# Spectral heads by a real transform's symmetry, and five low parts by transfers that add

## The reference, cut to what matters

```python
p = h @ w_in_ab[e]                        # 1024 -> 512 spectral + 512 conv + 512 gate
a4 = a.reshape(1, 256, 4, 128)            # 256 tokens, 4 heads of 128 features
f = jnp.fft.fft2(a4, axes=(1, 3), norm="ortho").real
y = jnp.einsum("bshd,hde->bshe", f, fnet_map)
```

## Time and profile before

| | us |
|---|---|
| median of 3 runs | 734.05 |
| lowest, highest | 733.32, 734.15 |
| span of the profiled execution, first to last instruction | 731.6 |
| run's median less that span | 2.45 |
| PE busy | 719.8 (98%) |
| DVE busy | 502.8 (69%) |
| ACT busy | 395.2 (54%) |
| POOL busy | 2.4 |

### The profile page before, as it was taken

One profiled execution on the slowest core, in us unless ns is written; L12 is line 12 of the kernel. 1 busy time (PEld: TensorE's weight loads), 2 busy tenths in 40 slices (PEclk: granted clock), 3 DMA queues, 4 the chain that ended last, 5 costly groups with the idle time before them and its releaser, 6 DMA issues.

```text
span 731.6 us, 9776 instructions
## 1 busy us (share of the span) xinstructions
PE 719.8 (98%) x3940; PEld 629.7 (86%) x3940; DVE 502.8 (69%) x801; ACT 395.2 (54%) x614; POOL 2.4 (0%) x8
## 2 busy tenths in 40 slices
PE   7999999999999999999999999999999999999996
PEld 6888889999999999888888888888888888888885
DVE  5879996998877889977744555555686445555544
ACT  3167446874886675658644434443666444344423
POOL 0000000000000000000000000000000000000000
PEclk9999999999999999999999999999999999999999
DMA  8999994798835343423755545554336555455201
GB/s 329 416 422 422 421 410 154 259 396 327 325 124 212 135 161 116 179 102 116 288 177 197 201 173 180 206 190 172 116 116 229 176 198 200 173 181 207 73 1 57
DMA packets 23085, 156.13 MB, mean 213 GB/s; under 512 B 2560, under 2 KB 2816, under 8 KB 5120
## 3 DMA queue, kind: packets, MB, share of 16 engines
q1 hardware_dynamic: 22464, 152.88, 55.2%
q0 software_dynamic: 576, 2.62, 0.9%
HBM read 154.44 MB, written 1.05 MB: 213 GB/s over the span
## 4 chain that ended last, share of the span: by engine, by line
PE 87%; DVE 6%; DMA 4%; ACT 2%; SPq 1%; issue 0%; ACTq 0%
PE pb L1601 22%; PE pb L1603 22%; PE pb L1602 21%; PE pb L1665 10%; DMA raw<-w_dram 4%; DVE raw L1032 3%; DVE w L1029 2%; PE pb L1894 2%; PE pb L2005 1%; PE pb L1758 1%; PE pb L1757 1%; PE pb L1759 1%; PE pb L2073 1%; PE pb L1927 1%; PE pb L1937 0%; PE pb L1872 0%
## 5 line engine op out<-in xcount | busy, mean ns | idle before, releaser
L1029 DVE TENSOR_TENSOR w<-raw,w 128x2048 fp32r<-128x2048 f32 x97 | 221.4, 2291 | 141.2 <-ACT w L629 141.2
L629 ACT ACTIVATE w<-raw 128x2048 fp32r<-128x2048 f32 x97 | 184.9, 1915 | 138.7 <-PE pb L1603 114.7
L1601 PE MATMUL pb<-w,r 128*128 128x512 f32 (+1 forms) x640 | 244.6, 382 | 0.0
L1603 PE MATMUL pb<-w,r 128*128 128x512 f32 (+1 forms) x640 | 241.1, 377 | 0.0
L1602 PE MATMUL pb<-w,r 128*128 128x512 f32 (+1 forms) x640 | 240.7, 376 | 0.0
L1603 PEld LDWEIGHTS pb<-w,r 128*128 128x128 f32 x640 | 120.4, 188 | 22.6
L1601 PEld LDWEIGHTS pb<-w,r 128*128 128x128 f32 x640 | 120.6, 188 | 21.2 <-issue 0.2
L1602 PEld LDWEIGHTS pb<-w,r 128*128 128x128 f32 x640 | 120.6, 188 | 21.0
L1601 PE MATMUL pb<-r,w 128*128 128x256 f32 x288 | 82.5, 287 | 0.4 <-DVE r L1029 0.4
L1603 PE MATMUL pb<-r,w 128*128 128x256 f32 x288 | 81.5, 283 | 0.0
L1602 PE MATMUL pb<-r,w 128*128 128x256 f32 x288 | 81.5, 283 | 0.0
(11 more groups left out here) (208 smaller groups left out, 673.6 us busy)
## 6 DMA issues: line engine op xcount, KB each, us to landing
raw<-w_dram SPq DMA_DIRECT2D x129, 1024.0 KB, 4.9
ow<-w_dram SPq DMA_DIRECT2D x8, 1024.0 KB, 15.3
ow<-w_dram SPq DMA_DIRECT2D x8, 512.0 KB, 16.9
oh<-w_dram SPq DMA_DIRECT2D x2, 1024.0 KB, 22.5
x<-x_dram SPq DMA_DIRECT2D x2, 512.0 KB, 5.3
f<-rc_dram POOLq DMA_DIRECT2D x1, 1024.0 KB, 5.6
acc<-row_dram POOLq DMA_DIRECT2D x2, 512.0 KB, 6.7
out_dram<-f SPq DMA_DIRECT2D x4, 256.0 KB, 2.3
```

Source lines behind the costliest of these rows:

```text
L629: return e.activation(out, in_, ACT.Copy, **kw)
L1029: return e.tensor_tensor(out, a, b, op)
L1601: e.matmul(out, a_hi, b_hi, start=start, stop=False)
L1603: return e.matmul(out, a_lo, b_hi, start=False, stop=stop)
```

## The change

- `cdsd` has 128 columns: rows 0 and 64 to 127 of the output (packed frequencies) are cosine columns, the others sine columns. "ac" is done for two heads a bank: 8 matmuls of 128 columns, 4 banks, 4 scaled copies.
- "f" has two regions in a bank, cosines and sines, of NS = 130 columns each: 16 matmuls of 130 columns. ACT takes partitions 0 to 63 from the sines, 64 to 127 from the cosines, and then partition 0 again from the cosines (waiting for the first copy): three copies a head.
- "fm" is two matmuls a head: the folded map by the 130 frequencies, and the other folded map by the frequencies in reverse order (126 columns).
- POOL loads the mirrored maps into the two `sqt` buffers and folds them with `sgn`: six operations of 128 x 256, at the place of the `dft` load.
- For slabs 26 to 30 ACT also writes the negated slab to the low half (a second copy), DVE's split is left out, and POOL adds the slab from DRAM to the low half by an accumulating DMA. The load ring waits for the negated copy (`s_minus`), PE for the transfer (`s_sum`).

```diff
-CSTS = [("ident", 128), ("mask", 384), ("cdsd", 256), ("fmap", 512)]
+CSTS = [("ident", 128), ("mask", 384), ("cdsd", 128), ("fmap", 512)]
...
+BY_DMA = [26, 27, 28, 29, 30]
+LOW_AT = {k: n + 1 for n, k in enumerate(k for k in range(len(MATS)) if k not in BY_DMA)}
...
         def _(e):
             e.wait_ge(s_mv, 12)
-            e.dma_start(acc[0][:, :], dft_d).then_inc(s_dft, 16)
+            e.dma_start(acc[0][:, :], dft_d[:, 0:4 * T]).then_inc(s_dft, 16)
+
+            e.wait_ge(s_na, 7)
+            for i in range(2):
+                e.dma_start(sqt[i][:, :], dft_d[:, 4 * T + i * T:5 * T + i * T]).then_inc(s_mir, 16)
+            sgn = V("sgn", 0)
+            e.wait_ge(s_vec, 16)
+            e.wait_ge(s_mir, 32)
+            for i in range(2):
+                e.tensor_scalar(sqt[i][:, :], sqt[i][:, :], sgn, None, MUL).then_inc(s_fold, 1)
+            e.wait_ge(s_cst, 16)
+            for i in range(2):
+                part = C("fmap", i * T, T)
+                e.wait_ge(s_fold, i + 1)
+                e.tensor_tensor(part, part, sqt[i][:, :], ADD).then_inc(s_fold, 1)
+            for i in range(2):
+                e.wait_ge(s_fold, 3 + i)
+                e.tensor_scalar(sqt[i][:, :], C("fmap", i * T, T), sgn, None, MUL).then_inc(s_fold, 1)
+
+            def low_sum(k):
+                e.wait_ge(s_minus, BY_DMA.index(k) + 1)
+                e.dma_start(W[(k + 2) % NSPL][:, 1, :], w_d[MATS[k]], accum_op=ADD).then_inc(s_sum[k], 16)
+
+            low_sum(26)
+            low_sum(27)
             e.wait_ge(s_flo, 4)
             e.dma_start(rc, rcnt_d).then_inc(s_rc, 16)
             e.dma_start(prow[:, :], row_d[0]).then_inc(s_prow, 16)
+            low_sum(28)
+            low_sum(29)
+            low_sum(30)
             e.wait_ge(s_cv3, 1)
...
                     copy(W[(k + 2) % NSPL][:, 0, 0:n], raw_of(i)[:, 0:n]).then_inc(s_hi, 1)
+                    if k in BY_DMA:
+                        copy(W[(k + 2) % NSPL][:, 1, 0:n], raw_of(i)[:, 0:n], scale=-1.0).then_inc(s_minus, 1)
...
-            for h in range(4):
+            for g in range(2):
                 for a in range(2):
-                    p.wait_ge(*ended("ac", h, a))
-                    copy(AC[:, h, a, :], out_of("ac", h, a), scale=rcol[:, 4 + a:5 + a]).then_inc(s_ac, 1)
+                    p.wait_ge(*ended("ac", g, a))
+                    copy(AC[:, g, a, :], out_of("ac", g, a), scale=rcol[:, 4 + a:5 + a]).then_inc(s_ac, 1)
             for h in range(4):
                 p.wait_ge(*ended("f", h))
-                copy(F2[:, 4 + h, :], out_of("f", h)).then_inc(s_f, 1)
+                cosines, sines = [bank_of("f", h)[:, o_:o_ + NS] for o_ in (0, T)]
+                copy(F2[0:64, 4 + h, 0:NS], sines[0:64, :]).then_inc(s_sin, 1)
+                copy(F2[64:128, 4 + h, 0:NS], cosines[64:128, :])
+                p.wait_ge(s_sin, h + 1)
+                copy(F2[0:1, 4 + h, 0:NS], cosines[0:1, :]).then_inc(s_f, 1)
                 if h < 3:
                     diagonals(2 * h, 2 * h + 1)
...
             def weights(k):
-                p.wait_ge(s_lo, k + 1)
+                if k in BY_DMA:
+                    p.wait_ge(s_sum[k], 16)
+                else:
+                    p.wait_ge(s_lo, LOW_AT[k])
...
-            for h in range(4):
+            for g in range(2):
                 for a in range(2):
-                    bank_free("ac", h, a)
-                    p.wait_ge(s_a, h + 1)
-                    e.matmul(out_of("ac", h, a), F2[:, h, a * P:(a + 1) * P], C("cdsd"), start=True,
-                             stop=True).then_inc(s_ps, 1)
+                    bank_free("ac", g, a)
+                    for b in range(2):
+                        h = 2 * g + b
+                        p.wait_ge(s_a, h + 1)
+                        done = e.matmul(out_of("ac", g, a)[:, b * P:b * P + P], F2[:, h, a * P:(a + 1) * P], C("cdsd"),
+                                        start=True, stop=True)
+                    done.then_inc(s_ps, 1)
             p.wait_ge(s_dft, 16)
             for h in range(4):
                 bank_free("f", h)
...
+                    p.wait_ge(s_ac, 2 * (h // 2) + a + 1)
+                    col = AC[:, h // 2, a, h % 2 * P:h % 2 * P + P]
+                    e.matmul(bank_of("f", h)[:, 0:NS], col, acc[0][:, a * T:a * T + NS], start=a == 0, stop=False)
+                    done = e.matmul(bank_of("f", h)[:, T:T + NS], col, acc[0][:, (2 + a) * T:(2 + a) * T + NS],
+                                    start=False, stop=a == 1)
                 done.then_inc(s_ps, 1)
+            p.wait_ge(s_fold, 6)
             for h in range(4):
                 bank_free("fm", h)
                 p.wait_ge(s_f, h + 1)
-                e.matmul(out_of("fm", h), C("fmap", h * P, P), F2[:, 4 + h, :], start=True,
+                e.matmul(out_of("fm", h)[:, 0:NS], C("fmap", h * P, P), F2[:, 4 + h, 0:NS], start=True, stop=False)
+                e.matmul(out_of("fm", h)[:, NS:T], sqt[h // 2][:, h % 2 * P:h % 2 * P + P], F2[:, 4 + h, T - NS:0:-1], start=False,
                          stop=True).then_inc(s_ps, 1)
```

More of the change, by code:

```diff
@@ L76 @@
     ("norm_mix_g_2", 16), ("norm_ffn_g_2", 16), ("conv_w_2", 124), ("conv_b_2", 4), ("conv_ln_g_2", 4),
-    ("conv_ln_b_2", 4), ("eps", 2),
+    ("conv_ln_b_2", 4), ("eps", 2), ("sgn", 1),
 ]
@@ L233, in outputs @@
         o.slab(24 + c, ("a", 2 * c + 1))
-    for h in range(4):
-        o.out(("ac", h, 0), ("ac", h, 1))
+    for g in range(2):
+        o.out(("ac", g, 0), ("ac", g, 1))
+    o.n += 4
     o.out(*run("f", 0, 1, 2, 3))
@@ L386, in two_block_program @@
             sem(f"s_{n}") for n in ("vec", "id", "xa", "xb", "cst", "dft", "rc", "prow", "frow", "out"))
-        s_hi, s_lo, s_mod, s_half = (sem(f"s_{n}") for n in ("hi", "lo", "mod", "half"))
+        s_hi, s_lo, s_mod, s_half, s_minus = (sem(f"s_{n}") for n in ("hi", "lo", "mod", "half", "minus"))
+        s_sum = {k: sem(f"s_sum{k}") for k in BY_DMA}
         s_ps = sem("s_ps")
@@ L413, in two_block_program @@
             sem(f"s_{n}") for n in ("b", "gpad", "col", "gt", "sg", "tap0", "tap", "a", "ac", "f", "fhi", "flo"))
+        s_mir, s_fold, s_sin = sem("s_mir"), sem("s_fold"), sem("s_sin")
         s_dg, s_dgm, s_cv3, s_lnm, s_lnv, s_lnc, s_lnq, s_lnr, s_lni, s_lnb, s_lnn, s_cs2, s_clo = (
@@ L433, in two_block_program @@
         PADW = T + 30
+        NS = T // 2 + 2
         G0 = F0[:, 0:4 * PADW].rearrange("p (k n) -> p k n", k=4)
@@ L602, in _ @@
                     n_mat += 1
-                    emptied.append((s_lo, n_mat))
+                    k = n_mat - 1
+                    emptied.append((s_minus, BY_DMA.index(k) + 1) if k in BY_DMA else (s_lo, LOW_AT[k]))
                     if n_mat == 6:
@@ L1076, in stream @@
                     at["mat"] += 1
+                    if k in BY_DMA:
+                        continue
                     w = W[(k + 2) % NSPL]
@@ L1876, in _ @@
                 bank_free("f", h)
-                out = out_of("f", h)
                 for a in range(2):
[L1879 to L1882, removed]
+                    p.wait_ge(s_ac, 2 * (h // 2) + a + 1)
[3 more added lines that the diff above has]
+                                    start=False, stop=a == 1)
                 done.then_inc(s_ps, 1)
+            p.wait_ge(s_fold, 6)
             for h in range(4):
@@ L2089, in constants @@
     d = np.arange(P)
-    ang = 2 * np.pi * ((d[:, None] * d[None, :]) % P) / P
-    put("cdsd", np.concatenate([np.cos(ang), np.sin(ang)], 1) / np.sqrt(P))
+    row = np.arange(P)
+    freq = np.where(row >= 64, row - 64, np.where(row == 0, 64, row))
+    ang = 2 * np.pi * ((d[:, None] * freq[None, :]) % P) / P
+    put("cdsd", np.where((row >= 64) | (row == 0), np.cos(ang), np.sin(ang)) / np.sqrt(P))
     s = np.arange(T)
@@ L2148 @@
     for name, n in VECS:
-        if name != "eps":
+        if name not in ("eps", "sgn"):
             vec[:, VOFF[name]:VOFF[name] + n] = a[name].reshape(n, P).T
@@ L2153 @@
     cst, dft, rc = constants()
-    cst[:, COFF["fmap"]:COFF["fmap"] + 512] = a["fnet_map_2"][0].transpose(1, 0, 2).reshape(P, 512)
+    row = np.arange(P)
+    vec[:, VOFF["sgn"]] = np.where((row >= 64) | (row == 0), 1.0, -1.0)
+    fmap, at = a["fnet_map_2"][0].transpose(1, 0, 2).reshape(P, 512), COFF["fmap"]
+    own = np.where(row >= 64, row - 64, np.where(row == 0, 64, row))
+    cst[:, at:at + 512] = fmap[own]
+    other = np.flatnonzero(row % 64)
+    mirror = np.zeros((P, 2 * T), np.float32)
+    mirror[other] = fmap[P - own[other]]
+    dft = np.concatenate([dft, mirror], 1)
     x = np.ascontiguousarray(a["x"][0].T.reshape(KT, P, T).transpose(1, 0, 2))
```

## The result

The changed kernel takes 741.38 us, the median of 4 runs (740.31 to 742.33); the kernel before takes 733.69 beside it. The ratio is 1.0101, with a 95% interval of 1.0087 to 1.0114: 7.7 us slower, where 1.7 was forecast, and 0.9 us above the range of the prediction. The direction, to which the prediction gave a chance of 0.50, was right, the size was not.

A forecast was written before the change was run, and what follows sets the result against it. PE bounds the kernel, busy 719.8 of 731.6 us. Saving 4.9 us, net 3.25 after ACT's and DVE's delays, then slab 30's transfer starts the feed-forward 1.7 us late: 734.05 + 1.7 = 735.8, range 731.7 to 740.5.

The forecast's parts named there:

- PE's own work: Spectral heads: narrower matmuls take PE from 12.1 to 7.15 us, saving 4.9 us if it never waits.
- First wait: First transform, heads 2 and 3: PE waits 0.8 us for ACT, delayed by negative slab copies; costs 0.85 us.
- Second wait: Heads' spectrum copies: ACT needs 1.15 us a head, PE 0.9; gain so far 3.7 us, 3.0 with copies at 0.26.
- DVE not the bound, and the tap tie: DVE loses five splits without effect; last tap sum ties with PE until slab 29's copy makes it 0.45 us late.
- Third wait: First feed-forward product: PE waits for slab 30's adding transfer, 9.35 us to landing, and starts 1.7 us late.
- the term for the neighbours of the transfer: Slab 30's transfer: half of slab 35's load, released by the same semaphore, adds 1.25 us.
- The term for the add itself: Slab 30's transfer: a plain 5.6 us plus one more stream of 2.5 for reading the destination.
- The upper end, 13.7: Longest landing of slab 30's transfer: two in series, 11.2 us, plus slab 35's load, 2.5.
- The clock: At the feed-forward start, a PE stall over 5 us could bring a lower-clock stretch; no size given.
- long: Rival: slab 30's transfer takes 13.7 us, the feed-forward step is 6.8 us late, time 740.5 or so; chance 0.09.
- hidden: Rival: slab 30's transfer lands in 5.5 us or less, time 732.0; chance 0.28, including a larger gain ahead of it.
- It cancels: Rival: slab 30's landing of 6.2 to 9.1 us puts the feed-forward step within 1.47 us of 338.12, about 734; chance 0.22.

The follow-up runs named there:

- the kernel with the symmetry alone: The changed kernel without any adding transfer, DVE splitting all slabs, only the transform's symmetry kept: 731.03 us, ratio 0.9961 to the kernel before.
- the kernel that keeps PE at work: The changed kernel with 16 overwritten products of 256 columns ahead of the first feed-forward product: 739.61 us, ratio 1.0079 to the kernel before.
- with the loads held: The changed kernel with slab 35's load and the last row's load held until slab 30's sum landed (slab 36's load thereby too): 736.6 us, one run.
- the kernel with the transfers alone: The kernel before plus the five adding transfers and ACT's negative copies, nothing of the transforms: 744.06 us, ratio 1.0136 to the kernel before.

## Why the prediction was wrong in size

**PE's own work: right.** In the kernel with the symmetry alone PE runs the first two stages without a wait, 8 matmuls of 128 columns (16 records) and 16 of 130:

```profile
281.35 1.95 PE L1915 MATMUL pb<-cst,f 128*128 128x128 f32 x16
283.13 0.39 PE L1924 MATMUL pb<-acc,f 128*128 128x130 f32 x2
...
286.71 0.39 PE L1932 MATMUL pb<-f,cst 128*128 128x130 f32 x2
```

That is 1.78 and 3.58 us, 0.22 a matmul; with 1.78 for the maps 7.14, where 7.15 was forecast, and 4.95 saved. The changed kernel has the waits in it:

```profile
280.86 1.06 PE L1920 MATMUL pb<-cst,f 128*128 128x128 f32 x8
282.67 1.13 PE L1920 MATMUL pb<-cst,f 128*128 128x128 f32 x8 [0.75 <-ACT f L664]
283.63 0.39 PE L1929 MATMUL pb<-acc,f 128*128 128x130 f32 x2
...
287.21 0.39 PE L1937 MATMUL pb<-f,cst 128*128 128x130 f32 x2
...
290.15 0.60 PE L1945 MATMUL pb<-f,acc 128*128 128x256 f32 x2
```

**First wait: right**, 0.75 us for 0.8; the first stage takes 2.77 us for 1.78, so it costs 1.0 for 0.85. **Second wait: mis-sized.** The maps take 2.94 us for 1.78, so it costs 1.2 us where the forecast's times give 0.35. ACT's timeline:

```profile
284.73 0.85 ACT L664 ACTIVATE f<-pb 64x130 f32<-64x130 f32 x3 [0.42 <-PE pb L1930]
285.49 0.68 ACT L664 ACTIVATE acc<-cst,vec 128x128 f32<-128x128 f32 x2
286.07 0.83 ACT L664 ACTIVATE f<-pb 64x130 f32<-64x130 f32 x3
```

A head's block is 0.76 us of copies (284.73 to 285.49) and 0.58 of diagonals, 1.34 and 1.32, not 1.15. Three copies of this small shape go 0.25 us apart, as fast as the 128-column rows and no faster: half the columns bought nothing here, and the prediction should have kept to the row it had. The diagonal products start at 290.15 instead of 292.8, 2.8 us gained when counted from the start of the stage, where 3.7 was expected and 3.0 was the stated low end.

**DVE not the bound, and the tap tie: right.** PE waits 0.3 us (0.45 predicted) for the tap sum. With adds for slabs 26 and 27 alone this wait is gone, and with them slab 29's negative copy, which the prediction blames; but with no add at all it is 0.3 too, from DVE's own splits.

**Third wait: right in place, and this is the step that failed: the term for the neighbours of the transfer.** ACT ends slab 30's negative copy at 331.5, where 330.45 was forecast, mostly by the second wait, and POOL issues at 331.81, 0.3 us behind it, for which the forecast had nothing: 1.35 us in all. The transfer takes 11.81 where 9.35 was taken: 2.45 us more. Slab 35's load was counted by half, 1.25, and takes 2.7 (as slab 29's transfer shows for the same pair), since the adding transfer moves nothing until that load is nearly through. Slab 36's load, issued while the transfer is under way, was put at nothing and takes 1.1. The term for the add itself was right in sum, 5.6 + 2.5 = 8.1 forecast and 8.0 measured once the neighbours are held, though by luck in its parts: it leaves 3.1 us in which nothing moves, and the packets move for 6.2 us of the 8.0. Start of the step: 339.85 forecast, 343.67 measured, which is 1.35 + 2.45 later. The upper end, 13.7, did cover the transfer. (The prediction says of its three waits "each time by ACT"; this one is for POOL's transfer, as its own later part has it.)

**The clock: named only in a rival, and not summed.** The prediction said that a stall of over 5 us "could bring a stretch at the lower level" and put no price on it. It cost 1.4 us, nearly as much as the forecast's whole net loss. Without it the profiled span would have been 5.5 us longer, inside the range; the kernel that keeps PE at work takes 739.61. The six microseconds between forecast and measurement (1.7 and 7.7) are then 1.35 for the later issue, 2.45 for the transfer, 1.4 for the clock, and 0.8 that the runs have more than the profiled spans. The range itself was cut short: the rival "long" had the step 6.8 us late, and 734.05 + 6.8 is 740.85, not the 740.5 at which the range ends.

The rival "hidden" falls with the landing (5.5 us or less was needed). "It cancels" put the landing at 8.1, which the prediction drew from the Trainium skill (Collectives: The Full Stack, "The bandwidth ceiling"). The landing alone, 8.0 us, agrees, but it was never alone here: two loads of 1 MB ran beside it. At 8.0, with the loads held, PE still started the step 1.6 us late (341.32 from a stage start of 282.33, against 338.12 from 280.70), because the lead ahead of it was smaller than assumed.

## What to carry to other kernels

Before work is moved from an idle-enough engine to a transfer, work out the room between the release of the source and the first use, slab by slab: three of the five had it, the fourth just not, the fifth cost 9 us, and only one or two were worth having. When costing a transfer, list everything that the same semaphore sets in motion, and every load that is issued before the transfer would land; here a load behind it on its own queue cost nothing, and those on the other queue cost 3.8 us. And a wait of several microseconds on PE is to be priced with the slow products behind it.

## What the runs showed that was not expected

- An accumulating transfer of 1 MB lands after 8.0 us with nothing beside it, 10.7 with one 1 MB load that starts with it, 11.8 with a second one on its way, and a mean of 15 for slabs 26 and 27, while three slab loads were under way. Beside a load that starts with it, it moves nothing for 4.5 us, where it begins after 1.5 alone.
- POOL spends 0.86 to 0.94 us to issue an adding transfer, 0.55 to issue a plain one of the same size.
- Copies of 64 x 130 and of 1 x 130 out of PSUM follow each other at 0.25 us on ACT, hardly faster than copies of 128 x 256 (0.27): at this size the count is the cost, not the columns.
- A stall of 3.4 us left the granted clock at 1.00; one of 7.2 us let it fall to 0.50 while PE stood still, and the products stayed slow for the first 2.7 us of work. In the kernel with the transfers alone, after a stall of 7.4 us, they stayed slow for 5.3.
